# Ten low-part subtractions of the key stretches put on GpSimd, between its key loads, in place of VectorE

## The chip, the core and the metric

One core of one Trainium2 chip runs the whole kernel. The metric is the device time of one execution in microseconds; the median of several runs is given. "The span" is the time from the first to the last instruction of the one execution that the profiler recorded.

## What is computed

One inference step of a decoder layer (`D_MODEL` 1024) for two groups of rows with the same weights: a prompt of 512 tokens and 8 samples of 8 tokens, 576 rows in all. Cut to what matters here:

```python
h = rmsnorm(x, norm_mix_g) @ w_in          # columns: q, k, v, iq, iw, ik, su, sv, ga, gb
o_a = attend(q, k, v, iq, iw, ik)          # top-k selection, then 8 heads x 128
o_b = gelu(su) * (w_causal @ rmsnorm(gelu(sv)) + b)
x = x + (sigmoid(ga) * (o_a @ w_branch_a) + sigmoid(gb) * (o_b @ w_branch_b)) @ w_out
y = x + (silu(gate) * val) @ w_down        # gate, val: causal conv of rmsnorm(x) @ w_up
```

For the samples, `attend` works on a paged cache: each of the 8 samples has 16 pages of 128 keys and values. The kernel computes the logits against all 2048 cached keys and masks out what top-k left out:

```python
logits = q @ cache_k[page_table].T * scale + bias       # then the mask, softmax
out = softmax(logits) @ cache_v[page_table]
```

## The kernel before

**High and low parts.** Products with weights are exact to about float32 by splitting: ScalarE copies a weight chunk `W` into `WH` in the rounded type float32r (`split_high`, line 1417, the copy at L1424), and then another engine computes the low part `WL = W - WH` in the place of `W` (`split_low`, line 598, the subtraction at L602). TensorE then takes three products per step: high times high, weight high times activation low, weight low times activation high (`products`, L1022 to L1024; for row tiles L1066 to L1068). A chunk is 128x2048 words (256 columns, eight steps of 128 rows). There are three slots for `W`/`WL` and two for `WH`. `chunk_list` names the chunks in the order of use; chunk n lies in slot n % 3 and n % 2.

A chunk is split one tile early: when the first tile of chunk n is started, the place `after(tile)` (`split_after`, line 609) splits chunk n + 1. ScalarE and the engine for the low part both do so from their own programs. The low part waits for `high_ready`, ScalarE's count of high parts. TensorE waits in `split` (line 1013) for the count of low parts: `low_count` (lines 592 to 596) gives each chunk a semaphore and a value. There are two such counts, one for GpSimd and one for VectorE. Before the change GpSimd does the eight chunks of `k` and `v` (`POOL_SPLITS`, line 591), VectorE all others.

**The sample attention and the side work.** The 8 samples are taken in two groups of four (`G` = 0, 1). Each group has a *key stretch* (16 key pages, `kp`), a softmax, and a *value stretch* (4 samples of 16 value pages). Beside this, TensorE works off the `side` list: the projections `ga`, `gb`, `su`, `sv`, cut by a fixed plan (`quota`, `part_at`, `side_at`, lines 158 to 186) into four or five steps behind each half of a key page, and one or two behind each value page. `side_at['K', G, kp]` lists the tiles that end behind page kp of group G.

**A key page.** It goes through four engines:
- GpSimd loads it in two halves (`load_keys`, L655): one indirect DMA brings half a page of four samples, 128x2048 words, 1 MB. Load n (n = 0 to 31 in each group) is half n % 2 of page n // 2. There are four buffers `KH`: load n waits (`key_freed`, line 563) until half n - 4 is transposed. These loads are all that GpSimd does in the stretch.
- VectorE transposes the half (`transposed`, L1920) into one of three buffers `KTB` (the first of them lies in the tile RB, the others in R, so every third transposition writes RB), and waits before that until TensorE is done with half n - 3.
- TensorE multiplies it with the queries: 64 matmuls of 64 columns per half (L1261) after one wait for `k_transposed`. Then come the side steps.
- VectorE adds bias and mask (`logits`, L1900), two pages behind, and takes maxima at pages 13, 14 and 15 (L1936, L1940, L1943).

So VectorE's program in page kp is: two transpositions, `logits(kp - 2)`, and then `splits('K', G, kp)`, the low parts of those chunks that start to be needed.

After the last key load of group 0, GpSimd waits until the last logits are out (`drained(pool, 'kl', 0, NPAGES - 1)`) and loads the mask of group 1 (L952).

## Time and profile before

| | |
|---|---|
| Median of 3 runs | 1463.35 us (1460.19 to 1463.64) |
| Profiled execution | 1462.85 us, of which the span is 1461.2 us |
| Mean granted TensorE clock | 0.972 |
| TensorE matmul busy | 1360.6 us (93%) |
| TensorE weight load busy | 1225.1 us (84%) |
| VectorE busy | 796.6 us (55%) |
| ScalarE busy | 416.3 us (28%) |
| GpSimd busy | 335.3 us (23%) |
| Low parts on VectorE, on GpSimd | 73, 8 |

The page also follows the chain of work that ended last: TensorE has 75% of it, VectorE 11%, DMA 4%, "issue" 4%, ScalarE 4%, GpSimd 1%. In the tables of waits, "A <- B" means that A's engine sat idle before A, and that B ended that wait; "issue" stands for idle time that nothing in the profile explains. Busy times are sums over one engine; a matmul's duration is longer than its distance to the next one, since matmuls overlap. PE is TensorE, PEld its weight loads, DVE VectorE, ACT ScalarE, POOL GpSimd; R, RB, LS, WL and so on are the program's names of tiles.

### The profile page before, as it was taken

The page shows a single profiled execution, that of the slowest core. Times are in us where ns is not written, and L with a number is a line of the kernel's source. Part 1 is how long each engine was busy: PE and PEld are TensorE (multiplying, and loading weights), DVE is VectorE, ACT ScalarE, POOL GpSimd, SP SyncE. Part 2 cuts the span into 40 slices and gives each one's busy share as a digit, 9 for nine tenths or more (in the row PEclk, how much of TensorE's full clock was granted, in tenths as well). Part 3 has the DMA queues.
Part 4 walks back from the last instruction along what each step waited for, and adds up shares of the span by engine and source line. Part 5 has one row for each costly group of instructions (what it writes and reads, how often), then busy time and mean ns, then how long its engine had stood idle before and what let it go on. Part 6 is the DMA issues. An engine that isn't in the chain of part 4 may idle for free.

```text
span 1461.2 us, 33775 instructions
## 1 busy us (share of the span) xinstructions
PE 1360.6 (93%) x14554; PEld 1225.1 (84%) x14554; DVE 796.6 (55%) x1141; ACT 416.3 (28%) x596; POOL 335.3 (23%) x427
## 2 busy tenths in 40 slices
PE   6989998999888899889999989999999999999997
PEld 4866698986777866678866788999999999999997
DVE  4378879817388710398710236444766666663221
ACT  4243313237411220011221221223433333332221
POOL 3513323337322100232000002222222222210000
PEclk8899999999999999999999998999999999999998
DMA  6414213231799799999789691232433322242222
GB/s 183 140 49 149 76 58 131 67 111 55 223 395 362 289 353 403 407 393 370 289 332 402 258 356 65 91 117 71 151 87 87 87 81 73 78 139 83 82 84 73
DMA packets 170624, 266.81 MB, mean 183 GB/s; under 512 B 19866, under 2 KB 136011, under 8 KB 161259
## 3 DMA queue, kind: packets, MB, share of 16 engines
q1 hardware_dynamic: 149275, 174.13, 35.4%
q0 software_dynamic: 14320, 78.22, 14.2%
q10 hardware_dynamic: 6880, 12.29, 2.4%
q8 instruction: 115, 1.88, 0.5%
q14 instruction: 34, 0.28, 0.1%
HBM read 240.30 MB, written 24.18 MB: 181 GB/s over the span
## 4 chain that ended last, share of the span: by engine, by line
PE 75%; DVE 11%; DMA 4%; issue 4%; ACT 4%; POOL 1%; SPq 1%; ACTq 0%; DVEq 0%; POOLq 0%
PE PS L1022 15%; PE PS L1024 14%; PE PS L1023 14%; PE PS L1261 5%; PE PS L1293 5%; PE PS L1066 3%; PE PS L1372 3%; PE PS L1370 3%; PE PS L1371 3%; DVE SR L1824 3%; DVE STG L1823 3%; PE PS L1067 2%; PE PS L1068 2%; DMA R<-in_cache_v 2%; PE PS L1172 1%
## 5 line engine op out<-in xcount | busy, mean ns | idle before, releaser
L1022 PE MATMUL PS<-xn_hi,WH 128*128 128x288 f32 (+1 forms) x1424 | 431.7, 303 | 11.3 <-issue 4.7
L1023 PE MATMUL PS<-xn_lo,WH 128*128 128x288 f32 (+1 forms) x1424 | 421.3, 296 | 1.7 <-issue 1.7
L1024 PE MATMUL PS<-xn_hi,WL 128*128 128x288 f32 (+1 forms) x1424 | 421.5, 296 | 0.6 <-issue 0.6
L1022 PEld LDWEIGHTS PS<-xn_hi,WH 128*128 128x128 f32 (+1 forms) x1424 | 267.9, 188 | 27.0 <-issue 13.4
L1023 PEld LDWEIGHTS PS<-xn_lo,WH 128*128 128x128 f32 (+1 forms) x1424 | 268.4, 188 | 2.8 <-issue 2.7
L1024 PEld LDWEIGHTS PS<-xn_hi,WL 128*128 128x128 f32 (+1 forms) x1424 | 268.3, 188 | 2.7 <-issue 2.7
L602 DVE TENSOR_TENSOR WL<-W,WH 128x2048 fp32r<-128x2048 f32 (+2 forms) x73 | 154.7, 2119 | 185.2 <-ACT WH L1424 185.1
L1424 ACT ACTIVATE WH<-W 128x2048 fp32r<-128x2048 f32 (+2 forms) x81 | 144.7, 1787 | 107.4 <-PE PS L1372 74.7
L1464 ACT ACTIVATE STG<-PS 128x576 f32<-128x576 f32 (+2 forms) x44 | 23.3, 530 | 344.4 <-PE PS L1024 210.0
L655 POOL DMA_INDIRECT R<-in_cache_k,KROW x64 | 64.4, 1007 | 235.1 <-PE PS L1293 97.6
L1066 PE MATMUL PS<-WH,xn_hi 128*128 128x256 f32 (+1 forms) x320 | 104.0, 325 | 3.1 <-ACT R L1563 3.1
L1920 DVE STREAM_TRANSPOSE R<-R 128x2048 f32<-128x2048 f32 x42 | 96.2, 2298 | 19.1 <-PE PS L1261 14.0
L1370 PE MATMUL PS<-G_hilo,WH 128*128 128x288 f32 x352 | 104.2, 296 | 0.0
L1372 PE MATMUL PS<-G_hilo,WL 128*128 128x288 f32 x352 | 103.7, 295 | 0.0
L1371 PE MATMUL PS<-G_hilo,WH 128*128 128x288 f32 x352 | 103.7, 294 | 0.0
L1001 POOL COPY STH<-CV 128x2 f32<-128x2 f32 x44 | 51.5, 1170 | 199.3 <-DVE CV L2057 199.3
L1293 PE MATMUL PS<-R,R 128*32 128x128 f32 x2176 | 88.9, 281 | 4.0 <-DMA R<-in_cache_v 4.0
L1067 PE MATMUL PS<-WL,xn_hi 128*128 128x256 f32 (+1 forms) x320 | 91.9, 287 | 0.0
L1068 PE MATMUL PS<-WH,xn_lo 128*128 128x256 f32 (+1 forms) x320 | 91.7, 286 | 0.0
L1662 ACT ACTIVATE CV<-CV,VT 128x592 f32<-128x592 f32 x44 | 38.9, 884 | 173.3 <-DVE CV L2057 173.3
L1066 PEld LDWEIGHTS PS<-WH,xn_hi 128*128 128x128 f32 (+1 forms) x320 | 59.0, 184 | 27.3 <-issue 27.3
L1961 DVE TENSOR_SCALAR R<-PS,ST 128x128 f32<-128x128 f32 x16 | 4.9, 345 | 131.8 <-PE PS L1293 131.8
(295 smaller groups left out, 2415.0 us busy)
## 6 DMA issues: line engine op xcount, KB each, us to landing
R<-in_cache_v SPq DMA_DIRECT2D x128, 512.0 KB, 7.6
W<-in_w_in SPq DMA_DIRECT2D x30, 1024.0 KB, 6.5
W<-in_w_up SPq DMA_DIRECT2D x44, 512.0 KB, 4.7
W<-in_w_down SPq DMA_DIRECT2D x16, 704.0 KB, 4.8
x_scratch<-xT SPq DMA_DIRECT2D x2, 2304.0 KB, 9.5
W<-in_w_branch_a SPq DMA_DIRECT2D x4, 1024.0 KB, 5.5
W<-in_w_branch_b SPq DMA_DIRECT2D x4, 1024.0 KB, 5.1
W<-in_w_out SPq DMA_DIRECT2D x4, 1024.0 KB, 5.2
```

Source lines behind the costliest of these rows:

```text
L602: e.tensor_tensor(WL[n % NW][:, 0:c], W[n % NW][:, 0:c], WH[n % NH][:, 0:c].bitcast(F32), ALU.subtract).then_inc(low_count[name][0], 1)
L1022: pe.matmul(out, hi[:, k, cols], x.hi_block(n)[:, tokens], start=first, stop=False)
L1023: pe.matmul(out, hi[:, k, cols], x.lo_block(n)[:, tokens], start=False, stop=False)
L1024: return pe.matmul(out, lo[:, k, cols], x.hi_block(n)[:, tokens], start=False, stop=last)
L1066: pe.matmul(out, xn1.hi_block(k)[:, t], hi[:, k, :], start=(k == 0), stop=False)
L1067: pe.matmul(out, xn1.hi_block(k)[:, t], lo[:, k, :], start=False, stop=False)
L1068: end = pe.matmul(out, xn1.lo_block(k)[:, t], hi[:, k, :], start=False, stop=(k == KT - 1))
L1293: last = pe.matmul(bank('o', G, b)[32 * j:32 * j + 32, HD * u:HD * u + HD], PTs[:, u, kp, 32 * j:32 * j + 32], page[:, HD * h:HD * h + HD] ...
L1370: pe.matmul(out, hi[:, k, :], gated(n, 0)[:, t], start=(n == 0), stop=False)
L1371: pe.matmul(out, hi[:, k, :], gated(n, 1)[:, t], start=False, stop=False)
L1372: last = pe.matmul(out, lo[:, k, :], gated(n, 0)[:, t], start=False, stop=(n == FB - 1))
L1424: act.activation(WH[n % NH][:, 0:c], W[n % NW][:, 0:c], ACT.Copy).then_inc(S_("high_ready"), 1)
```

## The change

The low parts of the ten chunks whose split falls into the key stretches are computed by GpSimd. `key_splits` lists them by group and page; worked out from the plan, these are:

| group, page | 0, 1 | 0, 5 | 0, 8 | 0, 12 | 0, 15 | 1, 1 | 1, 5 | 1, 8 | 1, 12 | 1, 15 |
|---|---|---|---|---|---|---|---|---|---|---|
| chunk | ga 2 | ga 3 | gb 0 | gb 1 | sv 0 | gb 3 | su 0 | su 1 | su 2 | sv 2 |
| behind the issue of load | 6 | 14 | 20 | 28 | 31 | 6 | 14 | 20 | 28 | 31 |

GpSimd computes the low part of page kp right behind the issue of load 2 kp + 4, and those of pages 13 to 15 behind both last loads. VectorE leaves the ten out. The low parts are counted by the engine that makes them. The chunks that are split ahead of the first key stretch, and those of the value stretches, stay with VectorE.

```diff
-        POOL_SPLITS = ('k', 'v')
+        key_splits = {}
+        for G in range(2):
+            for kp in range(NPAGES):
+                for tile in side_at['K', G, kp]:
+                    starts = [n for n, (name, _) in enumerate(chunk_list) if name[0] == tile[0]
+                              and tile == ((*name, 0) if name[0] == 'sv' else (name[0], 2 * name[1]))]
+                    for n in starts:
+                        key_splits.setdefault((G, kp), []).append(chunk_list[n + 1][0])
+        pool_names = [name for name, _ in chunk_list if name[0] in ('k', 'v')] + sum(key_splits.values(), [])
         low_count, counts = {}, [0, 0]
         for name, _ in chunk_list:
-            on_pool = name[0] in POOL_SPLITS
+            on_pool = name in pool_names
             counts[on_pool] += 1
...
-            for n in range(4, 2 * NPAGES):
-                load_keys(pool, 0, n)
+            def key_stretch(G, n):
+                load_keys(pool, G, n)
+                kps = () if n < 4 or n % 2 else ((n - 4) // 2,) if n < 30 else (13, 14, 15)
+                if n == 30:
+                    load_keys(pool, G, 31)
+                for kp in kps:
+                    for name in key_splits.get((G, kp), ()):
+                        split_low(pool, *name)
+
+            for n in range(4, 2 * NPAGES - 1):
+                key_stretch(0, n)
             drained(pool, 'kl', 0, NPAGES - 1)
...
-            for n in range(2 * NPAGES):
-                load_keys(pool, 1, n)
+            for n in range(2 * NPAGES - 1):
+                key_stretch(1, n)
...
-            after = split_after(lambda *name: split_low(dve, *name) if name[0] not in POOL_SPLITS else None)
+            after = split_after(lambda *name: split_low(dve, *name) if name not in pool_names else None)
```

## Rows read from the trace of the kernel before

**Rows 1.** Windows: stretch; busy of PE, PEld, DVE, ACT, POOL; clock; DMA, GB/s.

```profile
404.00:504.00 100.00, 87.11 (x2151) 78.02 (x2155) 86.41 (x68) 12.22 (x11) 22.70 (x24) 0.98 0.92 346
620.00:721.00 101.00, 89.12 (x2199) 79.93 (x2201) 89.17 (x69) 14.16 (x13) 24.77 (x25) 1.00 0.92 346
```

**Rows 2.** Waits of PE, 404 to 504 us: total, times, longest.

```profile
PE PS L1261 <- issue: 8.8, 8, 2.1
PE PS L1022 <- issue: 2.8, 2, 2.2
PE PS L1261 <- DVE R L1920: 0.7, 1, 0.7
```

**Rows 3.** Waits of PE, 612 to 722 us.

```profile
PE PS L1261 <- issue: 9.2, 10, 1.9
PE PS L1022 <- issue: 1.8, 1, 1.8
```

**Rows 4.** Timeline of PE, the train of half page 10, group 0.

```profile
427.74 0.98 PE L1261 MATMUL PS<-R 128*32 128x64 f32 x54
430.38 0.41 PE L1261 MATMUL PS<-R 128*32 128x64 f32 x10 [1.66 <-issue]
```

**Rows 5.** Groups of instructions on DVE, 404 to 504 us.

```profile
L1920 DVE STREAM_TRANSPOSE R<-R 128x2048 f32<-128x2048 f32 x19 | 43.7, 2303 | 13.1 <-PE PS L1261 8.1 <-DMA R<-in_cache_k,KROW 5.0
L1920 DVE STREAM_TRANSPOSE RB<-R 128x2048 f32<-128x2048 f32 x9 | 20.7, 2303 | 3.0 <-PE PS L1261 3.0
```

**Rows 6.** Groups of instructions on DVE, 621 to 721 us.

```profile
L1920 DVE STREAM_TRANSPOSE R<-R 128x2048 f32<-128x2048 f32 x19 | 43.6, 2299 | 6.0 <-PE PS L1261 5.9
L1920 DVE STREAM_TRANSPOSE RB<-R 128x2048 f32<-128x2048 f32 x9 | 20.7, 2301 | 4.2 <-PE PS L1261 4.1
```

**Rows 7.** All low parts, min/median/max ns on either engine.

```profile
L602 DVE TENSOR_TENSOR WL<-W,WH x73: 759/2280/2299, 20.5 to 1430.6; 128x2048 fp32r<-128x2048 f32 x56, 128x1408 fp32r<-128x1408 f32 x16, 128x576 fp32r<-128x576 f32 x1
L602 POOL TENSOR_TENSOR WL<-W,WH x8: 4586/4618/4630, 172.4 to 291.8; 128x2048 fp32r<-128x2048 f32 x8
```

**Rows 8.** Timeline of DVE, end of the key stretch of group 0.

```profile
499.50 2.29 DVE L602 TENSOR_TENSOR WL<-W,WH 128x2048 fp32r<-128x2048 f32 x1 [0.94 <-ACT WH L1424]
504.32 0.79 DVE L1900 SCALAR_TENSOR_TENSOR R<-PS,NBr,R 128x128 f32<-128x128 f32 x2 [0.84 <-PE PS L1261]
```

**Rows 9.** Timelines around key loads 20 and 21, group 0.

```profile
442.73 0.95 POOL L655 DMA_INDIRECT R<-in_cache_k,KROW  x1 [1.95 <-DVE R L1920]
445.53 1.91 ACT L1424 ACTIVATE WH<-W 128x2048 fp32r<-128x2048 f32 x1 [0.46 <-ACT STG L1464]
446.93 0.95 POOL L655 DMA_INDIRECT R<-in_cache_k,KROW  x1 [3.25 <-DVE R L1920]
458.21 2.31 DVE L1920 STREAM_TRANSPOSE RB<-R 128x2048 f32<-128x2048 f32 x1 [0.68 <-PE PS L1261]
467.81 1.10 PE L1261 MATMUL PS<-RB,R 128*32 128x64 f32 x64
```

**Rows 10.** Timelines around key load 21, group 1.

```profile
664.31 1.92 ACT L1424 ACTIVATE WH<-W 128x2048 fp32r<-128x2048 f32 x1 [0.46 <-ACT STG L1464]
685.64 1.12 PE L1261 MATMUL PS<-RB,R 128*32 128x64 f32 x64
```

**Rows 11.** Chain that ended last; timelines: from issue to landing of key loads.

```profile
389.02 13.11 DMA R<-in_cache_k,KROW
607.99 0.94 POOL L655 DMA_INDIRECT R<-in_cache_k,KROW  x1 [3.36 <-PE PS L1293]
616.77 2.31 DVE L1920 STREAM_TRANSPOSE RB<-R 128x2048 f32<-128x2048 f32 x1 [1.34 <-DMA R<-in_cache_k,KROW]
```

**Rows 12.** Timelines of POOL and DVE: instructions beside each other.

```profile
349.00 2.84 POOL L907 TENSOR_TENSOR R<-R,RB 128x256 f32<-128x256 f32 x1
395.24 2.25 DVE L602 TENSOR_TENSOR WL<-W,WH 128x2048 fp32r<-128x2048 f32 x1
395.59 2.73 POOL L655 DMA_INDIRECT R<-in_cache_k,KROW  x1 [1.25 <-DVE RB L1920]
```

## The prediction

> **What bounds the kernel now.** I read the page first, then the two key stretches alone. TensorE is busy in 93% of the span (the page's first part, in the table), so anything that VectorE gives up counts only where TensorE waits for it. The splits that move lie in two stretches of sixteen key pages: 404 to 504 us (sequence group 0) and 620 to 721 us (group 1). By the view of windows each of them has TensorE busy for 87 to 89 us, VectorE for 86 to 89, GpSimd for 23 to 25, the DMA engines at a share of 0.92, and TensorE at the granted clock 0.98 and 1.00, the 2.4 GHz level [rows 1]. Three resources are nearly full there, and the average can't say which one paces the rest. The waits can.
>
> TensorE's own list of waits has one entry for VectorE in group 0, 0.7 us, and none in group 1 from 612 us on. Nearly all of its idle time (8.8 + 2.8 us in group 0, 9.2 + 1.8 in group 1) stands under "issue", which is nothing that the profile shows [rows 2, 3]. These pauses lie inside a train of matmuls: 54 of the 64 of one half page run, then 1.66 us pass, then the other 10 [rows 4]. The code's wait for a transposed half stands ahead of the 64, so a late VectorE can't open a gap behind the 54th. In the other direction the waits are many: VectorE's transpositions stood idle for 8.1 + 3.0 us in group 0 and 5.9 + 4.1 in group 1 until TensorE had used a buffer, against 5.0 us for a key load in group 0 [rows 5, 6]. So TensorE paces both stretches, VectorE runs ahead of it by the three transposition buffers, and it waits there.
>
> **The change, part by part.**
>
> *Removed from VectorE.* Ten subtractions of 128x2048 at 2.28 us [rows 7], five per stretch: 11.4 us of its 100. The edit is worth on the end what TensorE waited for them: at most the 0.7 us of [rows 2], and that one is at the first half page of the window, whose transposition, at 402.1 us, had itself waited for its key load, the 13.11 us of [rows 11], so the split isn't in it. What VectorE saves becomes a longer wait for TensorE at the next transposition. At the end of a stretch, too, the last logits (504.32 us) had waited 0.84 us for TensorE [rows 8], behind the last of VectorE's splits; without it they wait longer for the same half page. I take 0. The bounds: no gain, or 2.28 us times ten, 22.8 us, were the "issue" pauses the splits' doing.
>
> *Added to GpSimd.* The same ten at 4.62 us, from its eight splits of the same form elsewhere [rows 7]: 46 us in all, beside the 47 us that it works in the two windows (22.7 + 24.8) [rows 1]. Its load is no limit. What counts is what stands behind the split on its queue: the next key load. Five splits per stretch hold a load: behind the issue of load 6, 14, 20, 28 and, after both last loads, behind 31, where GpSimd's next work waits for the last logits: the high part is there at 499.5, as VectorE's split shows, so GpSimd is done at 504.2, and the logits end at 505.1 [rows 8].
>
> *The new wait.* GpSimd now also waits for ScalarE's high part before it subtracts, with the next load queued behind. Behind loads 6, 14 and 28 the high part is there or comes shortly after the issue, and the next load is held by 3 us at most. The worst place is load 20 (page 8): it goes out at 442.73, 3 us before ScalarE even starts. There ScalarE runs from 445.53 to 447.44 us, the split ends at 447.44 + 4.62 + 0.2 = 452.3, and load 21, issued at 446.93 before, goes out 5.3 us later [rows 9]. In group 1 it is 664.31 + 1.92 + 4.62 + 0.2 = 671.1 [rows 10]. I follow this load, as it decides:
> - Load 21 feeds the transposition at 458.21 (the one into RB; every third goes there) and TensorE's half page at 467.81 [rows 9]. From the new issue to that matmul there are 467.8 - 452.3 = 15.5 us; the transposition takes 2.3 of them, so 13.2 us are left for the load. In group 1: 685.64 - 671.1 - 2.3 = 12.2 us [rows 10].
> - How long does a load take from issue to use? The trace shows it only where VectorE waited for one: 607.99 to 616.77, 8.8 us, with others ahead in the queue, and 13.1 us at the start of group 0, with the loads of the mask in the way [rows 11]. I take 8.8, since here the queue has at most one load ahead after so long a hold: margins of 4.4 and 3.4 us, no wait. By the upper end the margins are 0.1 and -0.9 us: plus 0.9 us in all.
> - Behind it loads follow one another, each as late as this one at first. The 28 transpositions of the 100 us [rows 5] make 3.6 us a half page, and the DMA engines have 8% to spare [rows 1], so the lateness shrinks slowly and the margin isn't used twice, save at load 28, where up to 3 us of hold may add to it. I put 0 to 2 us on that for both groups.
>
> *The shared port.* The bigger doubt is whether the split keeps its 4.62 us beside VectorE's work. Two rows show the two engines in each other's way: GpSimd's addition at 349.00 took 2.84 us, where its fellows take 0.7, and the issue of load 7 took 2.73 us in place of 0.95 [rows 9]; the second ran beside VectorE's split at 395.24, two SBUF operands, and ended only after that had ended, and in the timeline the first did the same with another [rows 12]. The Trainium skill, page "SBUF — State Buffer", section "Who interferes with whom", says that VectorE with two SBUF inputs and GpSimd reading SBUF exclude each other for a whole instruction, and that VectorE with one SBUF input leaves GpSimd alone. The first half agrees with 2.84 us; its inference that descriptor writing goes on beside such a subtraction does not agree with 2.73 us: by it load 7 would have been out after 0.95. In the key stretches VectorE now has transpositions (one SBUF input) and logits (one PSUM, one SBUF); no row shows GpSimd's arithmetic beside a transposition. With the subtraction gone, issues like that of load 7 lose their 1.8 us, which nobody waits for, as load 7 has three loads ahead. I take 4.62 us, with a doubled split as the other end.
>
> **The sum.** 0 (VectorE) + 0 (load 21, up to 0.9) + 0 to 2 (lateness carried on) + 0 (port, 4.62 us kept): with 0.3 for the carried part the profiled execution's 1462.85 us (its span of 1461.2 and 1.7 around it) becomes 1463.15. The median of the three runs shown, 1463.35, stands 0.5 above that execution, and they spread from 1460.19 to 1463.64, so the difference is within their noise. I forecast 1463.3 us.
>
> **The rivals.**
> *Slower: the hold reaches TensorE.* Place: load 21 of each group, then load 29. Mechanism: the split and VectorE's transpositions exclude each other, so that a split takes up to 4.62 + 2 x 2.3 = 9.2 us, 4.6 more. Load 21 goes out at 456.9 and 675.7. With 8.8 us to landing, TensorE's half pages come 0.2 and 1.2 us late; with 13.1 us, 4.5 and 5.5 [rows 9 to 11]. It decides from the point where issue plus landing exceeds 13.2 or 12.2 us. Price: 1.4 to 10 us, about 5.7 in the middle, 1469.0. For it: VectorE is busy for 86 of 100 us, so a split can't find a gap. Trainium skill, page "Perfetto Trace Analysis", section "Optimizing Scalar/DVE Operations", warns that moving work between these two engines may not help, as they share a port; here that would be this rival. Against it: the eight splits kept 4.59 to 4.63 us beside VectorE's other work [rows 7]. 0.15.
>
> *Faster.* The "issue" pauses (22.6 us by [rows 2, 3]) hang on something that the change relieves: the DMA engines, nearly full with key loads, also bring other things, and a held key load leaves them a gap of some 5 us; or the splits do open some of them. If a fifth goes, it is minus 5 us: 1458.3. For it: the pauses are there, and nothing in the profile explains them. Against: the places of the waits in the code don't fit them, and the bytes to be moved are the same. The full 22.8 us would need TensorE to wait for VectorE, which it doesn't. 0.19.
>
> *It doesn't do what it says.* The counts by which TensorE waits for low parts follow the list of chunks on either engine, and the order of the splits on GpSimd is that of the list; I see no way in which it fails, and any such case is in the forecast.
>
> **How the numbers follow.** The forecast (no change) has 0.66, slower 0.15, faster 0.19. A measurement of this kernel tells from no change what is over 0.3%, 4.4 us. The forecast's own range is 1460.5 to 1465.5: the carried part, plus the spread of the runs. To leave no more than 2 in 10 out I take in the likely end of each rival, to 1458.0 below and 1469.0 above.
>
> **What would show it.** In the changed profile: VectorE 22.8 us less busy and GpSimd 46 us more; ten splits on GpSimd of 4.6 us (right) or 6 to 9 us (the port); load 21 issued near 452.3 and 671.1; more VectorE idle time under TensorE, by some 20 us, and some under key loads; on TensorE's list VectorE's transpositions at 1 us or less per stretch (right) or several (the slower rival); "issue" pauses near 12 and 11 us, or fewer (the faster one). The forecast is wrong if TensorE's half pages from load 21 on start later than before by more than a microsecond against the stretch's start, or if either stretch ends over 2 us earlier.

## The result, and the profile after

| | before | after |
|---|---|---|
| Median of the runs taken side by side | 1462.6 us (8 runs) | 1470.48 us (8 runs, 1467.25 to 1485.02) |
| Ratio | | 1.0063, 95% interval 1.0035 to 1.0091 |
| Profiled execution: span | 1461.2 us | 1468.1 us |
| TensorE, VectorE busy | 1360.6, 796.6 us | 1367.5, 774.5 us |
| ScalarE, GpSimd busy | 416.3, 335.3 us | 416.5, 376.4 us |
| Mean granted clock | 0.972 | 0.967 |

The change is slower by 0.6%; the medians stand 7.9 us apart. I had forecast no change (1463.3 us). A second measurement of the same changed kernel gave 1.0056 (1.0029 to 1.0084), with medians 9.5 us apart.

What was moved has moved. Groups of the page (line, engine, operation, shapes, count, busy us, mean ns, idle time before), kernel after:

```profile
L610 DVE TENSOR_TENSOR WL<-W,WH 128x2048 fp32r<-128x2048 f32 (+2 forms) x63 | 131.9, 2093 | 181.5 <-ACT WH L1441 181.5
L663 POOL DMA_INDIRECT R<-in_cache_k,KROW x64 | 61.1, 954 | 205.5 <-PE PS L1310 97.9
L610 POOL TENSOR_TENSOR WL<-W,WH 128x2048 fp32r<-128x2048 f32 x18 | 82.8, 4599 | 104.9 <-ACT WH L1441 104.7
```

Ten splits left VectorE, and GpSimd's eighteen take 4.60 us each, as its eight did [rows 7]. Now the two key stretches by the views that stood ahead of the prediction: windows, TensorE's waits (408 to 509 and 616 to 730 us), and VectorE's groups (407 to 509 and 622 to 730 us). Group 0 stands before the dots, group 1 behind them.

```profile
407.00:509.00 102.00, 90.10 (x2104) 81.27 (x2105) 76.53 (x67) 12.23 (x11) 40.63 (x29) 0.95 0.91 336
622.00:730.00 108.00, 95.93 (x2347) 85.19 (x2336) 79.62 (x65) 14.16 (x13) 45.85 (x30) 1.00 0.89 329
```

```profile
PE PS L1278 <- issue: 8.6, 8, 2.4
PE PS L1039 <- issue: 3.3, 1, 3.3
...
PE PS L1278 <- issue: 9.4, 13, 2.4
PE PS L1039 <- issue: 1.3, 1, 1.3
PE PS L1040 <- issue: 1.1, 1, 1.1
```

```profile
L1937 DVE STREAM_TRANSPOSE R<-R 128x2048 f32<-128x2048 f32 x18 | 41.3, 2303 | 11.8 <-PE PS L1278 11.7 <-DMA R<-in_cache_k,KROW 0.2
L1937 DVE STREAM_TRANSPOSE RB<-R 128x2048 f32<-128x2048 f32 x9 | 20.8, 2307 | 11.1 <-PE PS L1278 11.0
...
L1937 DVE STREAM_TRANSPOSE R<-R 128x2048 f32<-128x2048 f32 x19 | 43.8, 2308 | 19.1 <-PE PS L1278 13.4 <-remote 3.0 <-DMA R<-in_cache_k,KROW 2.7
L1937 DVE STREAM_TRANSPOSE RB<-R 128x2048 f32<-128x2048 f32 x10 | 23.0, 2297 | 5.2 <-PE PS L1278 5.2
```

TensorE waits for nobody that the profile names, as before but for 0.7 us [rows 2, 3]; all it shows is "issue", 11.9 and 11.8 us, against 11.6 and 11.0 before. So these pauses hardly grew between the two traces: what grew is TensorE's busy time, by 6.9 us over the span, with the same matmuls (part of it at a lower clock, as follows). VectorE stands idle for TensorE longer than before [rows 5, 6], which is where its 22.1 us went. In group 1 a few keys come late for VectorE (2.7 us in all), and TensorE doesn't feel it. So neither the relieved engine nor the keys explain the loss, and yet the loss lies here: from TensorE's first to its last key matmul, group 0 takes 117.6 us in place of 115.1, group 1 114.2 in place of 110.4, 6.3 of the 6.9 us by which the span grew.

I divided these two stretches into the 64 *trains* (the 64 matmuls of a half page, first start to last start), and the rest. Trains: 83.4 us before, 87.6 after, so +4.1. Side steps: 117.9 and 120.5, +2.6. The way from one to the other: -0.4. Nearly all of the 2.6 us is in group 0, and there the trace shows a lower clock. Two stretches of the windows view of the kernel after, each right behind a pause of over 2 us:

```profile
451.00:455.00 4.00, 4.00 (x60) 3.69 (x58) 1.98 (x1) 0.00 (x0) 3.56 (x3) 0.58 0.82 319
...
482.00:486.00 4.00, 3.77 (x64) 3.61 (x68) 0.00 (x0) 0.00 (x0) 1.16 (x2) 0.62 1.01 398
```

TensorE had paused for 2.28 and 3.26 us; then the granted clock (the third figure from the end) was at the 1.2 GHz level for 3.4 us. In group 0 the kernel before has two such drops, the changed kernel four. One trace says little here, though. The two stretches together are at the 1.2 GHz level for 6.2 us in the kernel before and 19.7 us in the changed one; but in a second trace of the changed kernel (e3) it is 11.5 us, and there TensorE pauses for 2.28 and 2.43 us at the same two places with no drop behind either. And it is 16.7 and 22.6 us in e2 and e11 below, whose medians are those of the kernel before.

Where the train is lengthened can be seen at the place that I had followed, load 20 and 21 of group 0. Timeline (start, duration, instruction, idle time before), kernel after:

```profile
446.90 1.91 ACT L1441 ACTIVATE WH<-W 128x2048 fp32r<-128x2048 f32 x1 [0.46 <-ACT STG L1481]
448.89 4.56 POOL L610 TENSOR_TENSOR WL<-W,WH 128x2048 fp32r<-128x2048 f32 x1 [2.38 <-ACT WH L1441]
453.59 0.97 POOL L663 DMA_INDIRECT R<-in_cache_k,KROW  x1
454.00 1.19 PE L1278 MATMUL PS<-R 128*32 128x64 f32 x46
454.86 0.94 POOL L663 DMA_INDIRECT R<-in_cache_k,KROW  x1 [0.30 <-issue]
455.60 0.33 PE L1278 MATMUL PS<-R 128*32 128x64 f32 x6 [0.40 <-issue]
456.33 0.42 PE L1278 MATMUL PS<-R 128*32 128x64 f32 x12 [0.40 <-issue]
458.48 1.10 PE L1278 MATMUL PS<-R 128*32 128x64 f32 x64
```

The split ends, and the two loads that had queued up behind it go out 1.27 us apart. The train beside them goes in jerks (46, then 6, then 12 matmuls) and its last part starts 2.33 us after its first; the next train, with no issue at its start, runs its 64 in one piece. Only some 0.8 us of the first train is shown as idle: its 46 matmuls count as busy for 1.19 us, where all 64 of the next take 1.10. That is the lead which the experiments follow.

### The profile page after: what moved, and what is told of

It reads as the page before. It is cut to its first block, busy times and chain, and to the rows that moved or that the text cites. A ratio compares the mean times of both kernels' runs of the same rounds, so it can differ in the third digit from the quotient of the medians.

```text
span 1468.1 us, 33775 instructions
## 1 busy us (share of the span) xinstructions
PE 1367.5 (93%) x14554; PEld 1230.6 (84%) x14554; DVE 774.5 (53%) x1131; ACT 416.5 (28%) x596; POOL 376.4 (26%) x437
## 4 chain that ended last, share of the span: by engine, by line
PE 75%; DVE 10%; DMA 5%; issue 4%; ACT 3%; SPq 1%; POOL 1%; ACTq 0%; DVEq 0%; POOLq 0%
PE PS L1039 15%; PE PS L1041 14%; PE PS L1040 14%; PE PS L1278 5%; PE PS L1310 4%; DMA R<-in_cache_v 3%; PE PS L1389 3%; PE PS L1388 3%; PE PS L1387 3%; DVE SR L1841 3%; PE PS L1083 3%; DVE STG L1840 3%; PE PS L1084 2%; PE PS L1085 2%; PE PS L1243 1%
## 5 line engine op out<-in xcount | busy, mean ns | idle before, releaser
L1039 PEld LDWEIGHTS PS<-xn_hi,WH 128*128 128x128 f32 (+1 forms) x1424 | 269.9, 190 | 28.4 <-issue 14.9
L610 DVE TENSOR_TENSOR WL<-W,WH 128x2048 fp32r<-128x2048 f32 (+2 forms) x63 | 131.9, 2093 | 181.5 <-ACT WH L1441 181.5
L663 POOL DMA_INDIRECT R<-in_cache_k,KROW x64 | 61.1, 954 | 205.5 <-PE PS L1310 97.9
L610 POOL TENSOR_TENSOR WL<-W,WH 128x2048 fp32r<-128x2048 f32 x18 | 82.8, 4599 | 104.9 <-ACT WH L1441 104.7
L1310 PE MATMUL PS<-R,R 128*32 128x128 f32 x2176 | 88.9, 281 | 7.1 <-DMA R<-in_cache_v 6.4
```

The costliest lines, as they stand in the source:

```text
L610: e.tensor_tensor(WL[n % NW][:, 0:c], W[n % NW][:, 0:c], WH[n % NH][:, 0:c].bitcast(F32), ALU.subtract).then_inc(low_count[name][0], 1)
L1039: pe.matmul(out, hi[:, k, cols], x.hi_block(n)[:, tokens], start=first, stop=False)
L1310: last = pe.matmul(bank('o', G, b)[32 * j:32 * j + 32, HD * u:HD * u + HD], PTs[:, u, kp, 32 * j:32 * j + 32], page[:, HD * h:HD * h + HD] ...
```

## The experiments

Every kernel was run with the kernel before on the same chip (1463.4, 1464.9, 1463.5, 1464.4 and 1466.9 us in the five sets). "K" in the tables is the sum of both stretches, from first to last key matmul, and "trains" the part of it in the 64 trains, both from each kernel's profiled execution; before: K 225.5, trains 83.4. These two are weaker than the medians, as each comes from one execution: two traces of the kernel before (the other is e0) differ by 2.2 in K, two of the change (the other is e3) by 1.5 in K and 2.8 in trains. With e8 and e9 the profiled execution took some 8 us more than the median.

### Which part of the change costs

**e0, e3: both kernels again.** Nothing edited.

> The kernel before, once more, unchanged. It says how far two measurements of one kernel stand apart. Theory A (the change slows by what it does): ratio 1.000, within 0.002; clock of the span near 0.972; two or three stretches of 3.4 us at the lower clock in the sample attention; pauses of TensorE under 'issue' of 10 to 14 us per key stretch. Theory L (a lottery of pauses and clock, and the change only drew badly): the runs of this kernel spread as widely as those of the changed one (1467 to 1485), and its ratio may lie up to 0.006 off.

> The changed kernel once more, beside the kernel before on the same chip. Theory A: again 1.0035 to 1.009, with the clock of the span at 0.963 to 0.968 and more stretches at the lower clock than the kernel before has. Theory L: the ratio may as well fall to 1.000.

**e2: the ten low parts made by nobody.** TensorE takes the high part twice, as soon as ScalarE has made it.

```diff
-                        split_low(pool, *name)
+                    pass
...
-                return (blocks(WH[n % NH][:, 0:nk * width], nk), blocks(WL[n % NW][:, 0:nk * width], nk))
+                hi = blocks(WH[n % NH][:, 0:nk * width], nk)
+                return (hi, hi if name in sum(key_splits.values(), []) else blocks(WL[n % NW][:, 0:nk * width], nk))
```

> The ten low parts are made by nobody: TensorE multiplies with the high part in their place, after the count of high parts. VectorE is relieved as in the change, and GpSimd holds no key load. Theory hold: 0.998 to 1.001, clock 0.97 or above. Theory VectorE: 1.004 to 1.009, as the changed kernel. If VectorE had been worth something before: 0.99 to 0.995.

**e1: the hold alone.** VectorE keeps its splits. The six dummy subtractions took 6.9 us together, not the 4.7 that I had put, so this holds the queue longer than the change does.

```diff
-                        split_low(pool, *name)
+                        pool.wait_ge(S_("high_ready"), chunks[name][0] + 1)
+                        for _ in range(0 if kp == 15 else 6):
+                            link(pool.tensor_tensor(R3[:, 4096:4352], CST[:, 0:256], CST[:, 128:384], ALU.subtract))
```

> VectorE keeps its ten splits. GpSimd waits for the same high parts behind the same key loads and then does six linked subtractions of 128x256 (about 4.7 us) on constants, which nobody needs, ahead of the next key load (none behind load 31). Theory A, part hold (held key loads shift the DMA traffic and lengthen TensorE's pauses, which cost the clock): 1.004 to 1.009, as the changed kernel, with the clock near 0.967. Theory A, part VectorE (taking the splits off VectorE does it, by letting key loads go out earlier): 1.000. Theory L: anything within 0.006, without a pattern.

**e11: the wait alone.** As e1, without the loop.

> The kernel before with VectorE's splits kept, and only the wait for ScalarE's high part put on GpSimd at the ten places, with no arithmetic behind it. If the cost lies in the wait for the high part: 1467 to 1474, more than half of what the kernel with dummy work of 6.6 us showed (1480). If it lies in GpSimd's own 4.6 us: within 2 us of the kernel before, 1462 to 1466. The trace of the change shows GpSimd idle for 0 to some us ahead of a split, waiting for ScalarE, so I expect the smaller part here.

**e10: each split in two.** Half a split, the next load, the other half.

```diff
                 load_keys(pool, G, n)
+                for name in pending:
+                    split_half(pool, 1, *name)
...
-                        split_low(pool, *name)
+                        split_half(pool, 0, *name)
+                        pending.append(name)
```

> The changed kernel with each of the ten splits cut in two halves of 1024 columns (2.3 us each) with the next key load issued between them: the same arithmetic, but the queue held for 2.3 us twice in place of 4.6 us once (the wait for the high part stays ahead of the first half). If the length of the hold makes the cost: a third to two thirds of the cost comes back, 1465 to 1468. If any work on GpSimd between the loads costs, or the wait for ScalarE's high part is what holds: no change, 1469 to 1473.

| kernel | median, us | ratio to before, 95% interval | K | trains |
|---|---|---|---|---|
| e0 before again | 1465.45 | 1.0005 (0.9977 to 1.0033) | 223.3 | 83.7 |
| e3 change again | 1472.96 | 1.0056 (1.0029 to 1.0084) | 233.3 | 90.4 |
| e2 splits left out | 1463.63 | 1.0006 (0.9988 to 1.0025) | 228.5 | 86.7 |
| e1 hold of 6.9 us | 1480.38 | 1.0104 (1.0079 to 1.0128) | 242.6 | 98.7 |
| e11 wait for the high part | 1463.21 | 0.9991 (0.9963 to 1.0019) | 226.2 | 85.1 |
| e10 two holds of 2.4 us | 1467.00 | 1.0018 (0.9991 to 1.0045) | 228.3 | 87.1 |

Taking the splits off VectorE is worth nothing (e2); holding GpSimd's queue costs by itself, with VectorE not relieved (e1); the wait for ScalarE costs nothing (e11); and a shorter hold tends to cost less (e10, though its interval takes in both no cost and part of the change's). So what costs is what keeps GpSimd from its next key load: either the hold of the queue or GpSimd's arithmetic as such, which e1 still has. e16 and e17 below tell these two apart.

The trains alone can't carry this: e2 has 86.7 us in them, nearly as much as the change, at a ratio of 1.0006.

### How a held queue of loads reaches TensorE

The traces show a pattern. For each train (but the first of each stretch) of the fifteen traces with whole loads I noted whether a block of TensorE's instructions arrived in it (a packet of the "instruction" queue that ended 1.4 us before some moment of the train), and how many key loads GpSimd began to issue between 0.7 us before and 0.75 us after its start:

| instruction block | issues | trains | mean length, us | under 0.94 us |
|---|---|---|---|---|
| no | 0 | 476 | 0.90 | 454 |
| no | 1 | 119 | 1.54 | 8 |
| yes | 0 | 230 | 1.85 | 48 |
| yes | 1 | 99 | 2.14 | 0 |
| yes | 2 | 6 | 3.53 | 0 |

A train takes 0.88 us when it is left alone. Trains with the issue of a key load at their start are longer by 0.64 us on average, and those in which an instruction block arrives by 0.95 us. The second figure is no measure of what a block costs: a long train has more room for a block to arrive in. If only blocks count that arrive within 0.88 us of the train's start, trains without an issue take 1.07 us on average with a block and 1.22 without. The first figure stands without the blocks: 1.20 us for all trains without an issue and 1.83 for those with one. Two issues go with 3.5 us on average, most of them in e16; the change has such a train at 704.02 us, and it takes 2.35. The rest of the runs asks whether the issues are a cause, and what the blocks depend on.

**e4, e15: a wait that keeps issues off the trains, in the kernel before.**

```diff
             key_freed(e, G, n)
+            if n >= 6:
+                if n % 2:
+                    filled(e, 'kl', G, (n - 6) // 2)
+                else:
+                    e.wait_ge(S_("k_half_used"), 16 * G + (n - 6) // 2 + 1)
```

> The kernel before, with one more wait on GpSimd ahead of key load n (n from 6): until TensorE has ended its train of 64 key matmuls on half page n-6. The trains of the first six kernels (384 of them) gave the theory 'an issue at the start of a train': a train without an instruction refill takes 0.88 us, and 0.5 to 0.9 us more where GpSimd's issue of a key load begins between 0.5 us before and 0.7 us after the train's start; elsewhere the mean excess is 0.00 to 0.03 us. By it the wait moves each issue to 0.1 to 0.3 us after a train's end, 1.9 us or more ahead of the next: every train without a refill should be at 0.88 us, and the time 1.5 to 4 us below the kernel before (1459 to 1462 against 1463.4), more if the pauses at refills shrink too. Rival one, the transfers of the loads delay TensorE's instructions and it does not matter where the issue stands to a train: no change, within 1.5 us. Rival two, the extra wait makes keys late: VectorE's transpositions wait for keys and the time rises by 1 us or more.

> The kernel before with the wait for the end of train n-6, once more: the first time gave 0.9985 with an interval of 0.9963 to 1.0006. If the wait is a gain, the same side again, 1460 to 1462.5; if it was chance, 1463 or above.

**e5: the same wait in the changed kernel. e12: there, train n - 5 for the two loads behind a split.**

```diff
+                m = n - 5 if n in (7, 8, 15, 16, 21, 22, 29, 30) else n - 6
```

> The changed kernel with the same extra wait ahead of each key load. By the theory of the issue at the start of a train, the loads held behind a split no longer fall on a train unless they come late: most of the 6.5 us that the change costs comes back, so 1463 to 1466, and what is left is loads whose gate was open long before the split ended. By the rival that bursts of held loads (back to back issue, transfers together) cost the time, little comes back, 1468 to 1471, since after a 4.6 us split the gate of at least one load is open already. By the rival that GpSimd's subtraction itself disturbs TensorE: nothing comes back, 1470.

> The changed kernel with a wait for a train's end ahead of each key load: of half page n-6 as before, but of half page n-5 for the two loads behind each of the eight splits that lie between loads. By the theory of the queued issues (back to back issues behind a split fall on a train of key matmuls and stretch it) most of the cost goes: 1463 to 1467 against 1470 to 1473 for the change. Rival, the split itself or late issue costs: 1469 or more, and keys that come late would add to that.

**e6 and e7: each issue moved by dummy work.** After the wait of e4, two dummy subtractions ahead of the load (e6), or one ahead and one behind (e7).

```diff
+                for _ in range(2):
+                    pool_link[0](e.tensor_tensor(R3[:, 4096:4320], CST[:, 0:224], CST[:, 128:352], ALU.subtract))
```

> The kernel before with the wait for the train's end and then two linked subtractions of 128x224 (about 0.95 us each) in unused memory ahead of each key load from the sixth: as many issues as before, each some 2.0 us after the end of a train, so about at the start of the next (2.2 us after the end where two matmul steps of a side tile lie between). By the theory of the issue at the start of a train: some 40 of the 52 issues hit, 0.5 to 0.9 us each, 20 to 35 us, so 1483 to 1500. By the rivals (transfers, or their burst): the same loads 2 us later, 1462 to 1466. Should the loads come too late for the transpositions, VectorE shows a wait for keys; the kernel beside this one has the same work in another order.

> The same as the one beside it, but with one of the two dummy subtractions ahead of the load and one behind it: the same work on GpSimd, the issue 1 us earlier, about 1.1 us after a train's end and 1.1 us ahead of the next. By the theory of the issue at the start of a train: trains without a refill at 0.88 to 0.95 us, time 1460 to 1466. If the dummy subtractions cost by themselves, both kernels are slower by the same amount.

| kernel | median, us | ratio to before, 95% interval | K | trains |
|---|---|---|---|---|
| e4 before, gated | 1462.41 | 0.9985 (0.9963 to 1.0006) | 224.1 | 83.4 |
| e15 the same again | 1464.69 | 0.9993 (0.9972 to 1.0014) | 225.8 | 83.9 |
| e5 change, gated | 1469.41 | 1.0027 (1.0002 to 1.0051) | 235.4 | 94.0 |
| e12 change, gated later | 1474.49 | 1.0061 (1.0034 to 1.0089) | 231.6 | 88.9 |
| e6 two ahead of the load | 1465.84 | 1.0012 (0.9987 to 1.0036) | 225.4 | 83.4 |
| e7 one ahead, one behind | 1464.41 | 1.0003 (0.9980 to 1.0027) | 226.7 | 87.9 |

This went against my theory in its first form. I had it that each single issue on a train costs 0.7 us to the end, so e4 should gain and e6 lose 20 us or more. Neither happened; that e4 came out at 0.9985 was chance, as e15, the same kernel, has 0.9993. e6 did not do what it was meant to: its dummies took 0.80 us in place of the 0.95 that I had put, GpSimd fell behind its plan, and 21 of its 64 trains have an issue at their start. e4 has 13, against 23 in the kernel before, but its trains add up to 83.4 us all the same. The other trace of the kernel before (e0) has 13 such trains too, and 83.7 us; so the count moves by itself from one execution to the next, and with it nothing in the sum. e7 has 87.9 us in its trains and is no slower. The change has 11 such trains in one trace and 21 in the other (e3), so the number of single issues doesn't set it apart from the kernel before.

The gates in the changed kernel missed as well. For e5 I had expected 1463 to 1466; its median, 1469.4, lies between the two kernels, in the range that I had given to the rival that held loads leave in bursts, and it settles nothing. e12 spaces the first two loads behind a split by 2.8 us or more; at the eight places behind the splits five trains take 0.88, one 1.06, and the other two 2.09 and 3.18. For it I had expected most of the cost to go, and it costs as much as the change. Late keys don't explain that: VectorE waited 14.9 us for keys there, against 9.4 in the change, but TensorE's waits show only "issue", and in e6 VectorE waited 16.8 us for keys at a ratio of 1.0012. So with whole loads it is not shown that the burst is what costs.

**e8: half the bytes of each key load. e9, e14, e13: the same with the change, with the gate of e4, and with the change and the gate of e12.**

```diff
-            e.indirect_dma_start(out=KH[(n + 2) % 4], out_offset=None,
+            dst = KH[(n + 2) % 4] if n < 4 and not G else KH[(n + 2) % 4][:, 0:1024]
+            e.indirect_dma_start(out=dst, out_offset=None,
```

> The kernel before, but each key load from the fifth on brings only the first 1024 of the 2048 words of a partition (the second half of the key buffer keeps what it had, so the sample tokens' logits are of other keys): 4 KB a partition in place of 8, all instructions, waits and issues as they were. Theory of the refills: TensorE's instructions come in blocks of 16 KB by DMA; in the key stretches of the ten traces these blocks follow one another at 5 to 7 us while the DMA engines are at a share of 1.00, and at 3.4 to 3.9 us in the last 15 us of a stretch, where the key loads are over and TensorE shows no pause; so the transfers set TensorE's pauses. By it the pauses (20.7 and 16.5 us in excess of each half page's shortest time over the traces) fall by more than half, and the time by 15 to 35 us, 1428 to 1448. Rival, the issue at the start of a train: the issues stay where they are, only the stutter could change, so no more than 3 us, 1460 to 1464. Rival, VectorE's transpositions pace the stretch: no change.

> The changed kernel with the same halved key loads. If the hold on GpSimd's queue costs time through the transfers (a gap in the key queue, then a burst that crowds the instruction blocks), its cost of 6 to 9 us over the kernel before is gone or under 2 us once the transfers leave room: within 2 us of the other kernel with halved loads. If the hold costs through where the issues fall, or through clock drops that have nothing to do with the transfers, the difference of 6 to 9 us stays.

> The kernel before with halved key loads and the wait for the end of train n-6 ahead of each load. Its trains show 16.5 us of excess without the wait, about 12 of it beside an issue. Theory of the issues: each single issue moved off the trains gives back 0.7 us, so 3 to 7 us, 1435 to 1439. Rival, the pauses there are all those of the instruction blocks: 1441 to 1443.

> The same waits in the changed kernel with halved key loads, where the transfers leave room and keys cannot be late. The theory of the queued issues: its 7.6 us over the kernel before with halved loads fall to 3 us or less, 1440 to 1445. Rival, the cost lies in the split beside TensorE: it stays at 1447 to 1451.

**e16, e17: the queue held by a wait.** VectorE keeps its splits; GpSimd has no split, but four loads of each group wait for a train. e16 with whole loads, e17 with halved ones.

```diff
+            if n in (7, 15, 21, 29):
+                filled(e, 'kl', G, (n - 5) // 2) if (n - 5) % 2 else e.wait_ge(S_("k_half_used"), 16 * G + (n - 5) // 2 + 1)
+                pool_link[0](e.tensor_tensor(R3[:, 4096:4320], CST[:, 0:224], CST[:, 128:352], ALU.subtract))
```

> The kernel before, VectorE keeping its splits; key loads 7, 15, 21 and 29 of each group (those that stand behind a split in the change) wait for the end of the train of half page n-5 and for one dummy subtraction of 128x224 (0.95 us), so that they go out 1.2 us after that train and the next one or two right behind, 1.25 us apart, on the following train. The queue is held as long as in the change (some 5 us, eight times), with a fifth of its arithmetic. Theory of the held queue: 1468 to 1473, as the change. Rival, the subtraction itself beside TensorE: 1462 to 1465.

> The same holds with halved key loads, against 1441.7 for the kernel before with halved loads and 1449.3 for the change with halved loads. Theory of the held queue, by the issues that fall on a train: 1446 to 1450. Rival, the subtraction itself: 1441 to 1444.

| kernel | median, us | ratio to before, 95% interval | K | trains |
|---|---|---|---|---|
| e8 before, halved loads | 1441.68 | 0.9835 (0.9798 to 0.9871) | 207.1 | 72.8 |
| e14 the same, gated | 1443.95 | 0.9851 (0.9820 to 0.9883) | 203.6 | 69.0 |
| e9 change, halved loads | 1449.33 | 0.9886 (0.9844 to 0.9928) | 214.6 | 79.9 |
| e13 the same, gated later | 1446.26 | 0.9874 (0.9833 to 0.9915) | 207.6 | 73.8 |
| e17 held by a wait, halved loads | 1454.07 | 0.9921 (0.9889 to 0.9954) | 217.5 | 79.8 |
| e16 held by a wait, whole loads | 1481.15 | 1.0096 (1.0058 to 1.0133) | 240.7 | 98.9 |

*The blocks.* Halving the loads takes 22 us off by the medians; K is shorter by 18.4 us. TensorE's waits, 404 to 504 us of e8, answer to [rows 2]:

```profile
PE PS L1262 <- issue: 3.4, 5, 1.3
```

3.4 us in place of 11.6, with the same instructions and the same waits. Over both stretches such idle time is 8.9 us, against 26.2 and 21.3 in the two traces of the kernel before. So more than half of the "issue" pauses are an effect of the key transfers. The view of DMA shows by which way. Kernel before, 404 to 484 us (busy tenths of the DMA engines, then the queues with packets, MB, share of 16 engines), and its last part, 488 to 504 us:

```profile
DMA  9999999989999999999999999999998979999999
...
q0 software_dynamic: 3472, 25.28, 81.9%
...
q8 instruction: 13, 0.21, 1.0%
```

```profile
DMA  7883422200100000000200027999899999999999
...
q0 software_dynamic: 95, 0.65, 10.2%
...
q8 instruction: 4, 0.07, 1.6%
```

The queue "instruction" brings 16 KB at a time. That these are TensorE's instructions is read from their number: 115 packets in the span for 29,108 matmuls and weight loads, 253 each. While the key loads (q0) fill the engines, the blocks follow one another at 6.24 us (15 intervals from 395.1 to 488.8 us); once the loads are over and the engines mostly idle, the next two come 3.5 us apart, and there TensorE shows no pause. The 6.24 us alone prove nothing, as they are also the time in which TensorE uses a block up: 3881 matmuls and weight loads from 395 to 489 us are 258 in 6.24 us. What ties the pauses to the blocks is their place: in the kernel before, all 23 pauses of over 0.5 us inside the two stretches (behind their first key matmul) end 1.15 to 1.76 us after such a packet's end. The Trainium skill, page "Runtime: NRT & Kernel Launch", section "Instruction fetch mechanics", says that an engine's instructions come in blocks of 16 KiB, fetched while the last ones run, at a cost that is "mostly hidden". The size agrees; that it is hidden does not agree here, where the pauses end at the blocks and fall by more than half with the bytes of the key loads.

*The held queue.* e16 has no split on GpSimd, only eight holds with 0.67 us of arithmetic in each, and its ratio is 1.0096, no less than the change's. The holds came out longer than the change's: from the issue before to the issue of loads 7, 15, 21 and 29 it takes 8.2 us on average (6.5 in the change, 9.2 in e1, 3.4 in the kernel before), and it cost more than I had expected (1468 to 1473). The longer the hold, the more it costs: 1.0063 and 1.0056 for the change, 1.0096 for e16, 1.0104 for e1, with intervals that overlap. With halved loads, where the blocks have room, e17 is still slower than e8: 0.9921 against 0.9835, intervals apart. So a held queue costs without GpSimd's split, and nothing is left that speaks for the subtraction as such. And the place is where it was put. Timeline of e16, load 21 of group 0, and of e17, load 15:

```profile
456.01 0.97 POOL L660 DMA_INDIRECT R<-in_cache_k,KROW  x1 [0.70 <-POOL R L658]
456.18 0.54 PE L1267 MATMUL PS<-R 128*32 128x64 f32 x22
457.28 0.94 POOL L660 DMA_INDIRECT R<-in_cache_k,KROW  x1 [0.30 <-DVE R L1926]
457.38 1.01 PE L1267 MATMUL PS<-R 128*32 128x64 f32 x33 [0.66 <-issue]
458.53 0.94 POOL L660 DMA_INDIRECT R<-in_cache_k,KROW  x1 [0.30 <-issue]
458.82 0.32 PE L1267 MATMUL PS<-R 128*32 128x64 f32 x5 [0.43 <-issue]
459.56 0.22 PE L1267 MATMUL PS<-R 128*32 128x64 f32 x1 [0.42 <-issue]
460.27 0.43 PE L1267 MATMUL PS<-R 128*32 128x64 f32 x3 [0.50 <-issue]
```

```profile
428.36 0.96 POOL L661 DMA_INDIRECT R<-in_cache_k,KROW  x1 [0.27 <-POOL R L658]
428.99 1.00 PE L1268 MATMUL PS<-R 128*32 128x64 f32 x47
429.62 0.94 POOL L661 DMA_INDIRECT R<-in_cache_k,KROW  x1 [0.30 <-issue]
430.42 0.32 PE L1268 MATMUL PS<-R 128*32 128x64 f32 x4 [0.42 <-issue]
430.87 0.94 POOL L661 DMA_INDIRECT R<-in_cache_k,KROW  x1 [0.31 <-issue]
431.17 0.33 PE L1268 MATMUL PS<-R 128*32 128x64 f32 x6 [0.44 <-issue]
432.63 0.47 PE L1268 MATMUL PS<-R 128*32 128x64 f32 x7 [1.13 <-issue]
```

Three loads behind one hold, some 1.26 us apart, and a train of 4.2 and 3.8 us. The first of these two trains takes 1.81 us in the kernel before (at 452.73 us), the second 0.88 in e8. In e16 six of the eight trains behind holds are 2.8 to 3.3 us over 0.88, 17.8 us together, where the same six were 2.6 us over it before. That is 15.2 us, and K grew by 15.2: in this kernel the loss lies in these trains. By the profile 10.0 of the 15.4 us by which all its trains grew are busy time, not idle. Behind the second issue TensorE gets mostly one to seven matmuls at a time, with 0.4 us or more between; and the train, once drawn out, meets the next issue too. That this is why a burst costs what single issues don't fits these traces, but by which way an issue slows TensorE isn't shown. Nor are the change's bursts the same: of its eight holds two let three loads out within 1.3 us of each other and four others two, where in e16 six let out three.

With the loads halved, the change against e8 (e9) is the same picture: its trains are 7.1 us longer, K 7.5, the medians 7.65 apart (the intervals still overlap). So the cost is not one of crowded transfers alone. Keeping the held loads apart (e13) brought K back to e8's, 207.6 against 207.1, while its median came back by 3 of the 7.65 us and its ratio by 0.0012 of 0.0051, well inside the intervals. e14, the gate of e4 with halved loads, was to gain 3 to 7 us if single issues cost; it came out at 0.9851 against e8's 0.9835, so here too moving single issues gives nothing back.

*What stays open.* Shown is that the change's cost comes with the held queue: not from VectorE's relief (e2), not from the wait for ScalarE (e11), not from the subtraction (e16). Not shown is how the hold turns into the change's own 0.6%. In its first trace the trains have 4.1 of the 6.3 us in K and the side steps at a lower clock 2.6; in its second (e3) the trains have 7.0 of 7.8. With whole loads nothing that I tried gave the cost back beyond its interval, e12 least of all; the halves of e10 tend that way. Nor did I try anything that shows by which way GpSimd's issue slows TensorE's instructions. No version with whole loads beat the kernel before beyond its interval.

## Why the prediction was wrong

- *VectorE's relief is worth 0*: right. e2 has the relief and not the splits: 1.0006. In the changed kernel VectorE is 22.1 us less busy, and its transpositions stand idle under TensorE for 41.3 us in the two stretches in place of 21.1.
- *The split keeps 4.62 us*: right, 4.60 over all eighteen, 4.56 for the one shown. The slower rival, by mutual exclusion, is refuted in its mechanism; its time, 1469.0, was close by chance.
- *The worst hold is load 21*: right in place. It was issued at 453.59 us (forecast 452.3) and, in group 1, at 678.92 (671.1), a stretch that began 4.4 us later; ScalarE's high part came later there as well, at 674.1.
- *No key comes late for TensorE*: right. Its waits show VectorE nowhere in these windows.
- *So the hold costs nothing*: this is the step that failed. In the sum it is "0 (load 21, up to 0.9) + 0 to 2 (lateness carried on)". Under "The new wait" I priced the hold by one question, whether load 21 lands before its matmul. I followed the held loads down their queue to the data, and did not ask what else happens when they leave together. Measured: 7.9 us for the change, 14.2 for eight longer holds without any split (e16), with no matmul waiting for a key in either. There the time went into the trains beside which the held loads went out; for the change itself that way is only likely.
- *The "issue" pauses as a constant*: I had 22.6 us of idle time on the pacing engine that "nothing in the profile explains", and carried it over. Its size stayed near that, 23.7 us in the same two views after; over both whole stretches it is 26.2 and 21.3 us in the two traces of the kernel before and 25.5 and 26.8 in those of the change. What I had not seen is that TensorE can lose time that no wait shows: its busy time grew by 6.9 us with the same matmuls, and there my method of adding up waits had no term. The faster rival had the right source for the pauses (halved loads take more than half of them away), but a held load didn't lower them. That was 0.19 of chance on the wrong side; the slower side had 0.15.
- *The edges*: the range ended at 1469.0 for a median of 1470.5. It was built from key lateness alone, so it could not hold a cost of another kind.

## What to carry to other kernels

Price a hold on a queue by more than the question whether its data come late. Here no matmul waited for a key, and eight holds cost 8 to 14 us. Work put between the DMA issues of one queue lets what queued up leave in a burst; cutting it into pieces with an issue between them tended to cost less (e10), though that is within the noise. Look at busy time as well as at waits: a train of matmuls that is stretched shows mostly as busy, and it is found by comparing the same group of instructions, first start to last start, before and after. And take two traces of each kernel before reading a difference of a few us or a clock drop from one. Where pauses under "issue" stand on the pacing engine, look whether they end at packets of the instruction queue: here halved loads gave 22 us (with other results, as half the keys are missing), VectorE's 22 us gave nothing.

## What the runs showed of the hardware that I had not expected

- TensorE's instructions come by DMA beside the data: 16 KB per packet, 6.24 us apart with the engines full, 3.5 us apart with them mostly idle, and pauses of 0.5 to 3.3 us end 1.15 to 1.76 us after such a packet.
- A train of 64 short matmuls, which shares no data with the issue of an indirect DMA on GpSimd (0.94 us), takes 1.54 us on average in place of 0.90 if such an issue begins around its start (moving the issues away gained nothing: e4, e14, e15). With three of them, 1.26 us apart, ten such trains in the traces with whole loads take 3.7 us on average (1.25 to 4.6).
- The issue of load 7 had taken 2.73 us beside VectorE's split [rows 12]; with that split gone it took 0.96. In all traces together 36 issues of key loads begin while VectorE computes a low part: every one ends 0.81 to 0.84 us after that subtraction, and they take up to 2.93 us. Those that begin just before one take 0.94 to 0.96.
